# Matmuls of a zero tile ahead of the norm sums and of the grouped first chunks

## The chip, the cores and the metric

The kernel runs on one core of one Trainium2 chip. The time is the device time of one launch in microseconds. The kernel before takes 3053.3 us (median of three runs, 3047.53 to 3057.34). The traces come from single profiled executions.

## The reference, cut to what matters

Two transformer-like blocks of depth 2 over one sequence of 256 tokens and 1024 features, all in float32, one after the other.

```
first_block, for each of 2 layers:
  x = layer_norm(a * x + 0.5 * swiglu(x, w1, w3, w2))
  x = layer_norm(a * x + token_mixing(x))          # gMLP, short conv, MLA and NSA attention, 4 gates, w_o
  x = layer_norm(a * x + cross_attention(x, mem))  # 4 heads of 128, 256 memory rows
  x = layer_norm(a * x + 0.5 * swiglu(x, w1, w3, w2))

second_block, for each of 2 layers:
  x = x + 0.5 * swiglu(rmsnorm(x), w1, w3, w2)
  x = x + mixer(rmsnorm(x))       # layer 0: gated linear attention (GLA) + RG-LRU, layer 1: HGRN2
  x = x + 0.5 * swiglu(rmsnorm(x), w1, w3, w2)
  x = x + sigmoid(rmsnorm(x) @ ple_gate) * (p @ ple_proj)
x = rmsnorm(x)
```

So there are 8 norms with a mean (layer norms), and 9 without (root mean square), and 8 feed-forward networks of width 2816.

## The kernel before, in words

The five engines run five instruction streams that meet through semaphores. Activations lie with features on partitions: `X` is 8 chunks of 128 features by 256 tokens.

**Precision.** A product of float32 numbers is made of three matmuls: each operand is split into a high part (rounded to fp32r) and a low part (the rest), and high x high, high x low and low x high are summed (lines 395, 398, 399 in `three`, or 425, 428, 431 in `together`). `XH` and `XL` are the parts of the activations, `wh` and `wl` those of the weights; `BH` and `BL` hold other activations.

**The stream of weights.** SP loads blocks of 128x1024 into a ring of 6 (`raw`). For each block ACT writes the high part (line 998), POOL the low part in two halves (lines 360, 361, `lo_done`), into a ring of 4. TensorE's `weights()` waits for `lo_done`. The first matmul of a block tells ACT (`block_begun`) that an older one's place is free. A block is used by 24 matmuls.

**PSUM.** `R` has four banks, which `claim()` hands out in turn, waiting until the bank's chunk of four claims ago was taken (`bank_taken`). `Y` has the other four.

**A dense chunk** (`dense`): one block, 8 slices of the features, 3 matmuls each. **The first two or three chunks after a norm** are made by `together`: it waits for two or three blocks and claims as many banks, and then, slice by slice, waits for that slice of the activations (`ready(k)`) and multiplies it into all of them. It is called 18 times: at the start of the 8 feed-forward networks (2 chunks), of the 2 token mixers, the 2 cross attentions, and of the GLA and the HGRN mixer (3 chunks), at the output projections of these last two (3 chunks, from `BH`), and at the 2 gates with `ple_gate` (2 chunks).

**A norm.** TensorE sums over the partitions with a matrix of ones (`stats`, line 520; each such float32 matmul stands as two records in the trace). A norm with a mean has two sums: of `X`, whose result DVE subtracts (line 1664), and of the squares, which ACT writes (line 1091). A norm without has the second alone. Then ACT takes logarithm and exponential for the reciprocal root (lines 1082, 1083), DVE sharpens it (1655 to 1658), and for each of 8 slices DVE scales (1685), adds the bias where there is one (1693), ACT rounds the high part (1101) and DVE subtracts for the low part (1682), which releases `ready(k)`. `norm` on TensorE has places for work between: in the cross attention's norm two chunks of memory keys between the sums (`mem_keys`), more keys and the values behind them (`mem_values`); at the gates the projection of `p` behind the sum.

**Feed-forward.** `ffn` first writes zeros to the four banks of `Y` (line 490: matmuls of the zero tile `ZB`, 128x512 in bf16), then calls `together`, then loops over two up-projections and one down-projection per 128 hidden features. DVE adds the result to `X` (line 1640).

Each engine's order is that of the code; nothing is reordered by a scheduler.

Of the kernel before, what the change touches and what calls it, by code (L numbers as in the profile page):

```python
# [21 lines left out]
P = 128  # L22
# [23 lines left out]
Z_UP, UP_CHUNKS = 21, 14  # L46
Z_GATES = 4 * DC

RAW = 6
SPLIT = 4  # L50
BODY = 12
# [150 lines left out]
def build_program(nc, stream, small, table, masks, mix_w, mix_b, wcmp, x_in, mem_in, p_in, out):  # L202
# [4 lines left out]
    with ctx:  # L207
        def sb(name, shape, dt=F32):
            return ctx.enter_context(nc.sbuf_tensor(name, shape, dt))

        def sem(name):
            return ctx.enter_context(nc.semaphore(name))

        raw = sb("raw", [P, RAW, 1024])
        wh = sb("wh", [P, SPLIT, 1024], F32R)
# [19 lines left out]
        ZB = sb("ZB", [P, 512], BF16)  # L235
# [21 lines left out]

        raw_landed = [sem(f"raw_landed{i}") for i in range(RAW)]
        hi_done, lo_done, block_begun = sem("hi_done"), sem("lo_done"), sem("block_begun")
# [73 lines left out]
        def _(sp):  # L333
# [3 lines left out]
            sp.dma_start(X[:, :, :], x_in).then_inc(x_landed, 16)  # L337
            for n in range(RAW):
                sp.dma_start(raw[:, n, :], stream[n]).then_inc(raw_landed[n], 16)
            trips = (NB - RAW) // RAW  # L340
            with sp.Fori(0, trips) as it:
                for j in range(RAW):

                    sp.wait_ge(lo_done, it * RAW + (j + 1))
                    sp.dma_start(raw[:, j, :], stream[it * RAW + (RAW + j)]).then_inc(raw_landed[j], 16)
# [28 lines left out]
        def _(pe):  # L374
# [3 lines left out]
            def claim():  # L378

                m = t.n["chunk"]  # L380
                t.up("chunk")
                b = m % RING
                if m >= RING:
                    pe.wait_ge(bank_taken[b], t.value(("round", b)))
                t.up(("round", b))
                return R[:, b, :]

            def weights():
                n = t.n["block"]
                pe.wait_ge(lo_done, t.up("block"))  # L390
                return n % SPLIT
# [23 lines left out]
            def together(n, hi, lo, ready):  # L415

                slots, outs = [], []
                for _ in range(n):
                    slots.append(weights())
                    outs.append(claim())  # L420
                for k in range(DC):
                    ready(k)
                    for j, (s, o) in enumerate(zip(slots, outs)):
                        w = (slice(None), s, slice(k * P, k * P + P))
                        i = pe.matmul(o[:, 0:T], wh[w], hi[:, k, :], start=k == 0, stop=False, skip_group_check=True)  # L425
                        if k == 0 and j == 0:
                            i.then_inc(block_begun, 1)
                        i = pe.matmul(o[:, 0:T], wh[w], lo[:, k, :], start=False, stop=False, skip_group_check=True)  # L428
                        if k == DC - 1 and j > 0:
                            i.then_inc(block_begun, 1)  # L430
                        i = pe.matmul(o[:, 0:T], wl[w], hi[:, k, :], start=False, stop=k == DC - 1, skip_group_check=True)  # L431
                        if k == DC - 1:
                            i.then_inc(chunk_ready, 1)
# [52 lines left out]
            def ffn(ready):  # L486

                for b in range(4):

                    pe.matmul(Y[:, b, :], ZB[:, 0:P], ZB[:, :], start=True, stop=False, skip_group_check=True)  # L490

                def up_pair():
                    dense(XH, XL)
                    dense(XH, XL)

                def down(f, end=None):
                    from_dve()
                    s = weights()
                    for c in range(DC):
                        three(Y[:, c // 2, (c % 2) * T:(c % 2) * T + T], (slice(None), s, slice(c * P, c * P + P)),  # L500
                              HH[:, f % 2, :], HL[:, f % 2, :], False, False, begins=c == 0,
                              end=end if c % 2 == 1 else None)

                together(2, XH, XL, ready)
                with pe.Fori(0, (FC - 2) // 4) as it:
                    t.enter(it, {"block": BODY, "chunk": 8, dve_pe: 4, **{("round", b): 2 for b in range(RING)}})
                    for j in range(4):
                        up_pair()
                        down(j)
                    t.leave((FC - 2) // 4)  # L510
                up_pair()
                down(FC - 2)
                down(FC - 1, end=y_ready)

            def stats(n, wait):

                o = claim()
                for c in range(n[0]):
                    wait(c)
                    i = pe.matmul(o[:, 0:T], ONES, n[1](c), start=c == 0, stop=c == n[0] - 1, skip_group_check=True)  # L520
                i.then_inc(chunk_ready, 1)

            def norm(n, src, mean, wait=None, centring=None, scaling=None):
                if mean:
                    stats((n, src), wait)
                if centring is not None:
                    centring()
                stats((n, lambda c: W8[:, c, :]), lambda c: from_act())
                if scaling is not None:
                    scaling()  # L530
# [53 lines left out]
            def mixer(l):  # L584
# [90 lines left out]
                def aside(c):  # L675
# [39 lines left out]
                    if c == 32:  # L715
                        token_mix()

                together(3, XH, XL, split_ready)
                for c in range(3, Z_N):
                    dense(XH, XL)  # L720
# [27 lines left out]
            def cross():  # L748
                together(3, XH, XL, split_ready)
                dense(XH, XL)  # L750
                from_act()
                attention([cross_unit(h) for h in range(4)], lambda u: None)
                from_dve()
                first = t.n["chunk"]
                for _ in range(4):
                    dense(BH, BL, k_tiles=4)
                return first
# [1620 lines left out]
```

## Time and profile before

| | |
|---|---|
| median of three runs | 3053.3 us |
| the three runs | 3047.53, 3053.3, 3057.34 us |
| the profiled execution | 3047.86 us |
| its span, first to last instruction | 3046.1 us |
| mean granted clock of TensorE | 0.968 |
| TensorE busy | 2811.2 us, 92% |
| POOL, DVE, ACT busy | 2195.0, 1392.3, 1380.0 us |

The granted clock is 1.00 at 2.4 GHz and 0.50 at 1.2 GHz; it has these two levels in this trace, and the mean tells how much of the span was at which. A busy time of TensorE counts records whose ends are modelled and which overlap, so the distance from start to start tells the rate, not the length of one record. In a timeline the bracket behind an instruction is the idle time of its engine just before it, and what ended it; an instruction without a bracket followed its predecessor.

### The profile page before, as it was taken

The page shows a single profiled execution, that of the slowest core. Times are in us where ns is not written, and L with a number is a line of the kernel's source. Part 1 is how long each engine was busy: PE and PEld are TensorE (multiplying, and loading weights), DVE is VectorE, ACT ScalarE, POOL GpSimd, SP SyncE. Part 2 cuts the span into 40 slices and gives each one's busy share as a digit, 9 for nine tenths or more (in the row PEclk, how much of TensorE's full clock was granted, in tenths as well). Part 3 has the DMA queues.
Part 4 walks back from the last instruction along what each step waited for, and adds up shares of the span by engine and source line. Part 5 has one row for each costly group of instructions (what it writes and reads, how often), then busy time and mean ns, then how long its engine had stood idle before and what let it go on. Part 6 is the DMA issues. An engine that isn't in the chain of part 4 may idle for free.

```text
span 3046.1 us, 59381 instructions
## 1 busy us (share of the span) xinstructions
PE 2811.2 (92%) x21920; PEld 2687.0 (88%) x21920; DVE 1392.3 (46%) x2271; ACT 1380.0 (45%) x2018; POOL 2195.0 (72%) x1680
## 2 busy tenths in 40 slices
PE   6999999978999999999979998998799899988997
PEld 6999988868998989898868997997799899888996
DVE  3345424644345344524544344347533633654335
ACT  3444444444444444455444444445444544555444
POOL 6976655655996966565746986977699599766994
PEclk9999999999999999899999998999899999999998
DMA  5544433433554544343424553543355355433551
GB/s 206 186 166 145 136 120 123 139 111 110 181 184 140 179 145 163 125 138 112 146 90 132 182 169 118 182 156 125 119 189 181 123 187 180 151 127 133 187 185 63
DMA packets 122403, 451.83 MB, mean 148 GB/s; under 512 B 13586, under 2 KB 13586, under 8 KB 121364
## 3 DMA queue, kind: packets, MB, share of 16 engines
q1 hardware_dynamic: 120960, 441.43, 43.7%
q10 hardware_dynamic: 1300, 8.39, 0.7%
q8 instruction: 102, 1.67, 0.2%
q14 instruction: 41, 0.34, 0.0%
HBM read 448.72 MB, written 1.05 MB: 148 GB/s over the span
## 4 chain that ended last, share of the span: by engine, by line
POOL 58%; issue 30%; PE 9%; DVE 1%; POOLq 1%; ACT 1%; DVEq 0%; ACTq 0%
POOL wl L361 29%; POOL wl L360 29%; PE R L395 2%; PE R L398 2%; PE R L399 2%; PE R L520 1%; PE Y L395 1%; PE Y L398 1%; PE Y L399 1%; POOLq L366 0%; DVE W L1685 0%; PE R L425 0%; PE R L428 0%; PE R L431 0%; DVE XL L1682 0%
## 5 line engine op out<-in xcount | busy, mean ns | idle before, releaser
L360 POOL TENSOR_TENSOR wl<-raw,wh 128x512 fp32r<-128x512 f32 x836 | 1105.0, 1322 | 824.1 <-ACT wh L998 810.3
L998 ACT ACTIVATE wh<-raw 128x1024 fp32r<-128x1024 f32 x836 | 883.5, 1058 | 814.6 <-PE R L395 489.9
L395 PE MATMUL R<-XH,wh 128*128 128x256 f32 x4216 | 1216.5, 289 | 13.3 <-POOL wl L361 6.0
L398 PE MATMUL R<-XL,wh 128*128 128x256 f32 x4216 | 1201.6, 285 | 0.0
L399 PE MATMUL R<-XH,wl 128*128 128x256 f32 x4216 | 1200.9, 285 | 0.0
L361 POOL TENSOR_TENSOR wl<-raw,wh 128x512 fp32r<-128x512 f32 x836 | 1136.4, 1359 | 0.0
L395 PEld LDWEIGHTS R<-XH,wh 128*128 128x128 f32 x4216 | 817.4, 194 | 30.4 <-issue 14.7
L398 PEld LDWEIGHTS R<-XL,wh 128*128 128x128 f32 x4216 | 817.6, 194 | 1.7 <-issue 1.0
L399 PEld LDWEIGHTS R<-XH,wl 128*128 128x128 f32 x4216 | 817.1, 194 | 0.0
L395 PE MATMUL Y<-BH,wh 128*128 128x256 f32 x1408 | 400.0, 284 | 0.9
L398 PE MATMUL Y<-BL,wh 128*128 128x256 f32 x1408 | 399.2, 284 | 0.0
L399 PE MATMUL Y<-BH,wl 128*128 128x256 f32 x1408 | 399.2, 284 | 0.0
L1580 DVE SCALAR_TENSOR_TENSOR M<-M,R 128x256 f32<-128x256 f32 x176 | 74.2, 421 | 561.8 <-ACT M L1056 560.5
L395 PEld LDWEIGHTS Y<-BH,wh 128*128 128x128 f32 x1408 | 270.8, 192 | 2.5 <-DVE BL L1584 2.5
L399 PEld LDWEIGHTS Y<-BH,wl 128*128 128x128 f32 x1408 | 270.8, 192 | 0.0
L398 PEld LDWEIGHTS Y<-BL,wh 128*128 128x128 f32 x1408 | 270.8, 192 | 0.0
L1584 DVE TENSOR_TENSOR BL<-W,BH 128x256 fp32r<-128x256 f32 x176 | 247.1, 1404 | 6.0
L1582 DVE SCALAR_TENSOR_TENSOR W<-M,R 128x256 f32<-128x256 f32 x176 | 74.2, 422 | 327.9 <-PE R L399 327.6
L1056 ACT ACTIVATE M<-R 128x256 f32<-128x256 f32 x176 | 67.4, 383 | 294.6 <-PE R L399 277.8
L425 PE MATMUL R<-XH,wh 128*128 128x256 f32 x304 | 101.9, 335 | 89.1 <-DVE XL L1682 51.0
L395 PE MATMUL R<-BH,wh 128*128 128x256 f32 x544 | 159.4, 293 | 16.3 <-ACT M L1129 5.2
L1583 DVE CAST BH<-W 128x256 fp32r<-128x256 f32 x176 | 168.5, 957 | 6.0
(359 smaller groups left out, 3188.4 us busy)
## 6 DMA issues: line engine op xcount, KB each, us to landing
raw<-in_stream SPq DMA_DIRECT2D x836, 512.0 KB, 3.3
G<-in_wcmp ACTq DMA_DIRECT2D x2, 2048.0 KB, 7.6
G<-in_mem ACTq DMA_DIRECT2D x2, 1024.0 KB, 6.3
TB<-in_table SPq DMA_DIRECT2D x1, 1312.0 KB, 6.3
X<-in_x SPq DMA_DIRECT2D x1, 1024.0 KB, 8.6
out_dram<-X ACTq DMA_DIRECT2D x1, 1024.0 KB, 3.9
WS<-in_mix_w ACTq DMA_DIRECT2D x2, 256.0 KB
G<-in_p ACTq DMA_DIRECT2D x2, 256.0 KB, 2.6
```

What stands on the lines that cost most here:

```text
L360: pool.tensor_tensor(wl[:, s, 0:512], raw[:, r, 0:512], wh[:, s, 0:512].bitcast(F32), ALU.subtract)
L361: pool.tensor_tensor(wl[:, s, 512:], raw[:, r, 512:], wh[:, s, 512:].bitcast(F32), ALU.subtract).then_inc(lo_done, 1)
L395: i = pe.matmul(o, wh[w], hi, start=start, stop=False, skip_group_check=True)
L398: pe.matmul(o, wh[w], lo, start=False, stop=False, skip_group_check=True)
L399: i = pe.matmul(o, wl[w], hi, start=False, stop=stop, skip_group_check=True)
L425: i = pe.matmul(o[:, 0:T], wh[w], hi[:, k, :], start=k == 0, stop=False, skip_group_check=True)
L998: act.activation(wh[:, n % SPLIT, :], raw[:, n % RAW, :], ACT.Copy).then_inc(hi_done, 1)
L1056: give_dve(act.activation(EB[:, j % 2, :], o[:, 0:T], ACT.Tanh, scale=0.5))
L1580: take(stt(e, e, 1.0, o[:, 0:T], ALU.add, ALU.mult), m)
L1582: take(stt(h, e, 0.5 * scale, o[:, 0:T], ALU.mult, ALU.mult), m)
L1583: step(dve.tensor_copy(HH[:, b, :], h))
L1584: give_pe(tt_(HL[:, b, :], h, HH[:, b, :].bitcast(F32), ALU.subtract))
```

## The change

Two places on TensorE get matmuls that multiply the zero tile by itself. In `together`, behind the waits for the weights and the claims of the banks and ahead of the first `ready(k)`, there are 14 of them, into the first claimed bank. In `stats`, behind the claim and ahead of the wait for the first operand, there are 4, into the claimed bank. Each streams 512 columns of bf16. The first real matmul into a bank starts a new sum, so nothing of them remains. `KEEP_BUSY` is the number for `together`.

```
+KEEP_BUSY = 14
...
                 for _ in range(n):
                     slots.append(weights())
                     outs.append(claim())
+                for _ in range(KEEP_BUSY):
+
+                    pe.matmul(outs[0], ZB[:, 0:P], ZB[:, :], start=True, stop=True, skip_group_check=True)
                 for k in range(DC):
                     ready(k)
...
                 o = claim()
                 for c in range(n[0]):
+                    if c == 0:
+                        for _ in range(4):
+                            pe.matmul(o, ZB[:, 0:P], ZB[:, :], start=True, stop=True, skip_group_check=True)
                     wait(c)
                     i = pe.matmul(o[:, 0:T], ONES, n[1](c), start=c == 0, stop=c == n[0] - 1, skip_group_check=True)
```

Lines behind the insertions move: 395 to 399 become 396 to 400, 425, 428, 431 become 429, 432, 435, line 490 becomes 494, and 520 becomes 527. The new matmuls are on lines 424 and 525.

TensorE's order at the end of the first feed-forward network and through the first norm, before. `TB` holds the matrix of ones, `W8` the squares; what an instruction waits for stands behind it.

```order
L399 MATMUL Y<-BH,wl 128x256
L520 MATMUL R<-X,TB 128x256 [waits dve_pe,bank_taken0]
L520 MATMUL R<-X,TB 128x256 [waits dve_pe] x7
L520 MATMUL R<-W8,TB 128x256 [waits act_pe,bank_taken1]
L520 MATMUL R<-W8,TB 128x256 [waits act_pe] x7
L425 MATMUL R<-XH,wh 128x256 [waits lo_done,bank_taken3,bank_taken0,dve_pe,bank_taken2]
L428 MATMUL R<-XL,wh 128x256
L431 MATMUL R<-XH,wl 128x256
```

The same place with the change:

```order
L400 MATMUL Y<-BH,wl 128x256
L525 MATMUL R<-ZB 128x512 [waits bank_taken0]
L525 MATMUL R<-ZB 128x512 x3
L527 MATMUL R<-X,TB 128x256 [waits dve_pe] x8
L525 MATMUL R<-ZB 128x512 [waits bank_taken1]
L525 MATMUL R<-ZB 128x512 x3
L527 MATMUL R<-W8,TB 128x256 [waits act_pe] x8
L424 MATMUL R<-ZB 128x512 [waits bank_taken3,lo_done,bank_taken0,bank_taken2]
L424 MATMUL R<-ZB 128x512 x13
L429 MATMUL R<-XH,wh 128x256 [waits dve_pe]
L432 MATMUL R<-XL,wh 128x256
L435 MATMUL R<-XH,wl 128x256
```

The waits for banks and weights have moved from the first real matmul to the first of the zero tile; the first real one keeps the wait for its operand alone.

TensorE's order at the output projection of the GLA mixer with the change (before, the first matmul of `BH` has all these waits, and follows the last one of `XH` at once):

```order
L396 MATMUL R<-XH,wh 128x256
L399 MATMUL R<-XL,wh 128x256
L400 MATMUL R<-XH,wl 128x256
L424 MATMUL R<-ZB 128x512 [waits bank_taken2,lo_done,bank_taken3,bank_taken1]
L424 MATMUL R<-ZB 128x512 x13
L429 MATMUL R<-BH,wh 128x256 [waits outs_split]
L432 MATMUL R<-BL,wh 128x256
L435 MATMUL R<-BH,wl 128x256
```

Here too the fourteen stand behind `lo_done` of the third block and ahead of the wait for the activations, `outs_split`.

## Rows read from the trace of the kernel before

**Rows 1.** The page: busy time, share of the span and instructions of each engine.
```profile
PE 2811.2 (92%) x21920; PEld 2687.0 (88%) x21920; DVE 1392.3 (46%) x2271; ACT 1380.0 (45%) x2018; POOL 2195.0 (72%) x1680
```

**Rows 2.** Waits of TensorE: waiting line, releaser: us in total, times, longest.
```profile
PE R L425 <- DVE XL L1682: 51.0, 20, 5.3
PE R L425 <- POOL wl L361: 27.7, 3, 10.3
```

**Rows 3.** Line 490's instructions: duration ns least/median/greatest, first and last start.
```profile
L490 PE MATMUL Y<-ZB x32: 378/379/632, 9.6 to 2787.5; 128*128 128x512 bf16 x32
```

**Rows 4.** Timeline: start us, us, engine, line, operation, count [idle before <-releaser].
```profile
9.62 1.87 PE L490 MATMUL Y<-ZB 128*128 128x512 bf16 x4 [9.62 <-ACT CMSK L1463]
...
2424.66 1.03 PE L490 MATMUL Y<-ZB 128*128 128x512 bf16 x4
```

**Rows 5.** Timeline of TensorE in the first norm, behind the first feed-forward network.
```profile
217.90 3.62 PE L520 MATMUL R<-X,TB 128*128 128x256 f32 x16
222.64 3.94 PE L520 MATMUL R<-W,TB 128*128 128x256 f32 x16 [1.13 <-ACT W L1091]
...
231.85 0.56 PE L425 MATMUL R<-XH,wh 128*128 128x256 f32 x1 [5.28 <-DVE XL L1682]
```

**Rows 6.** Timeline of TensorE in the norm ahead of the cross attention.
```profile
618.91 3.62 PE L520 MATMUL R<-X,TB 128*128 128x256 f32 x16
...
628.11 1.24 PE L520 MATMUL R<-W,TB 128*128 128x256 f32 x5
```

**Rows 7.** Timeline of ACT and TensorE in a norm without a mean.
```profile
2377.88 3.56 ACT L1091 ACTIVATE W<-X 128x256 f32<-128x256 f32 x8
...
2378.44 3.75 PE L520 MATMUL R<-W,TB 128*128 128x256 f32 x16 [0.28 <-ACT W L1091]
```

**Rows 8.** Timeline where weights or a bank come last, or nearly.
```profile
656.51 0.55 PE L425 MATMUL R<-XH,wh 128*128 128x256 f32 x1 [10.26 <-POOL wl L361]
...
2148.31 1.71 POOL L361 TENSOR_TENSOR wl<-raw,wh 128x512 fp32r<-128x512 f32 x1
...
2150.71 0.55 PE L425 MATMUL R<-BH,wh 128*128 128x256 f32 x1 [15.08 <-DVE BL L1629]
...
2394.00 0.36 PE L425 MATMUL R<-XH,wh 128*128 128x256 f32 x1 [1.53 <-ACT M L1129]
```

**Rows 9.** Stretches: us, busy time of each engine (count), PEclk, DMA share, GB/s.
```profile
656.50:661.40 4.90, 4.89 (x23) 4.90 (x24) 0.00 (x0) 1.06 (x1) 2.50 (x2) 0.50 0.35 107
661.40:667.50 6.10, 6.10 (x53) 6.10 (x53) 0.00 (x0) 0.64 (x2) 0.00 (x0) 1.00 0.28 89
```

**Rows 10.** Timeline inside a feed-forward group behind a norm with a mean.
```profile
725.63 0.39 PE L425 MATMUL R<-XH,wh 128*128 128x256 f32 x1 [0.39 <-DVE XL L1682]
...
727.00 0.39 PE L425 MATMUL R<-XH,wh 128*128 128x256 f32 x1 [0.39 <-DVE XL L1682]
```

**Rows 11.** Timeline of TensorE at the start.
```profile
25.41 0.55 PE L425 MATMUL R<-XH,wh 128*128 128x256 f32 x1 [13.92 <-DVE XL L2163]
```

**Rows 12.** A stretch behind it, in the first group.
```profile
26.50:29.90 3.40, 3.40 (x18) 3.40 (x18) 0.00 (x0) 0.00 (x0) 0.00 (x0) 1.00 0.04 17
```

**Rows 13.** Timeline of the first chunks of the GLA mixer.
```profile
2048.90 0.55 PE L425 MATMUL R<-XH,wh 128*128 128x256 f32 x1 [4.56 <-DVE XL L1682]
...
2057.11 1.29 POOL L361 TENSOR_TENSOR wl<-raw,wh 128x512 fp32r<-128x512 f32 x1
...
2059.85 0.28 PE L395 MATMUL R<-XH,wh 128*128 128x256 f32 x1
```

**Rows 14.** Timeline of TensorE, the sum of the last norm.
```profile
3026.62 5.38 PE L520 MATMUL R<-W,TB 128*128 128x256 f32 x16 [2.39 <-ACT W L1091]
```

**Rows 15.** A stretch inside that sum.
```profile
3026.80:3030.20 3.40, 3.40 (x9) 2.69 (x9) 0.00 (x0) 2.62 (x7) 0.00 (x0) 0.50 0.02 5
```

**Rows 16.** Stretches in a token mixer, around small matmuls of the compressed attention.
```profile
343.94:347.35 3.41, 3.41 (x30) 3.19 (x29) 0.90 (x4) 0.47 (x1) 2.75 (x3) 1.00 0.73 240
347.35:350.77 3.42, 3.42 (x17) 3.28 (x17) 0.90 (x4) 0.05 (x1) 0.00 (x0) 0.50 0.43 155
```

More of the change, by code:

```diff
@@ L47 @@
 Z_GATES = 4 * DC
+KEEP_BUSY = 14
 RAW = 6
@@ L420, in together @@
                     outs.append(claim())
+                for _ in range(KEEP_BUSY):
+                    pe.matmul(outs[0], ZB[:, 0:P], ZB[:, :], start=True, stop=True, skip_group_check=True)
                 for k in range(DC):
@@ L518, in stats @@
                 for c in range(n[0]):
+                    if c == 0:
+                        for _ in range(4):
+                            pe.matmul(o, ZB[:, 0:P], ZB[:, :], start=True, stop=True, skip_group_check=True)
                     wait(c)
```

## The prediction

> **What bounds the kernel now.** I read the page's engine line first: TensorE is busy for 2811.2 of 3046.1 us, POOL for 72%, DVE and ACT for less than half [rows 1]. In the feed-forward stages the matmuls follow each other without a gap, so time lost there by TensorE is lost to the kernel. Then the waits of TensorE: the first matmul of the "together" groups (line 425) waits 51.0 us in 20 waits for the low part of the activations, and 27.7 us in three waits for POOL's low part of the weights [rows 2]. Those idle times are where the new matmuls are meant to stand. Then, group by group in the timeline, two questions: what ended the wait, and does TensorE or another engine set the pace behind it.
>
> **What is added.** 352 matmuls of a 128x512 bf16 zero tile: 14 in each of 18 together groups, 4 in each of 25 sums over the features. Nothing is removed, no other engine gets an instruction. The kernel has 32 matmuls of exactly this form (line 490), 379 ns each by the record [rows 3]; a row of four takes 1.03 us at full clock and 1.87 us at its start at the low one [rows 4], so one more costs (1.03 - 0.38) / 3 = 0.217 us, and cold about (1.87 - 0.63) / 3 = 0.41 us, with the longest record of [rows 3] for the last. Four cost 0.87 us warm, fourteen 3.0 us warm and 5.8 us cold.
>
> **The sums, by kind.** (a) Eight sums of the chunks before a mean is taken off, with no idle time ahead: TensorE comes straight from its last projection, and the sum runs at its own rate, 3.62 us for 16 records [rows 5, 6]. The four matmuls stand on the path, and DVE, ACT and the second sum wait for the result. 8 x 0.87. The two sums of squares behind the memory keys (628.1 and its twin in layer 1) also start with no idle time [rows 6], 2 x 0.87. Together 8.7 us. (b) The other six sums of squares start after 1.13 us of idle time [rows 5]; 0.87 us fits: 0. If a hand-over eats that cover, 0.2 us each. (c) Six sums of the root-mean-square norms start 0.28 us after TensorE stops, and ACT's squares set the pace: eight in 3.56 us from 2377.88, the sum 3.75 us from 2378.44 [rows 7]. Last squares end at 2381.44. The added four can be issued at about 2378.0, the sum then starts at 2378.87 and its 3.62 us end at 2382.5 and some hundredths, instead of 2382.19: with the drain about 0.45 us later. 6 x 0.45 = 2.7 us. (d) The first such norm, after 10.8 us of idle time, now issues its four only when DVE is done; its sum runs cold anyway. I take 0, between -1 and +1.
>
> **The together groups.** The code waits for the two or three blocks of weights and for the banks, then issues the fourteen, then waits for the activations. So all depends on which wait ended last. In six of the 18 groups the weights or a bank come last, or nearly: 656.5, its twin at 1561 and the HGRN output projection at 2757.4 are released by POOL; the gates at 2394.0 and 2999.5 by ACT emptying a bank; at 2150.7 the activations came last, but POOL's third block was done only at 2148.31 + 1.71 = 2150.02 [rows 8]. There the long idle time holds nothing: the fourteen start when the real ones would have. Behind them TensorE sets the pace: 72 matmuls, 23 of them at clock 0.50 in 4.90 us, 53 at clock 1.00 in 6.10 us, 0.213 and 0.115 us apart [rows 9]. The time at the low clock after the start stays, but part of it is now spent on zeros, so what is lost is their warm price, 3.0 us; at 2150 0.2 us less for the earlier start. 5 x 3.0 + 2.8 = 17.8 us. The upper bound is the cold price with nothing given back, 5.8 each where the group starts cold (four groups): 11 us more. The lower bound is that the low clock ends so much sooner by phase that a group gets back its 1.5 to 2 us: some 7 us less. I take 17.8, which the count of rows gives.
>
> In the other twelve the activations come last, 3.6 to 5.3 us after TensorE stopped [rows 5], and later still at the start; 3.0 us fit: 0, and the idle time falls to 0.6 to 2.3 us. The clock, which falls to 0.50 in most of them, should then mostly stay. But what is that worth? Behind a norm with a mean the group still waits 0.39 us for DVE at 725.63 and again at 727.00 [rows 10]: DVE's steps of 1.37 us a slice are longer than 9 warm matmuls (1.04) and than 6 cold ones (1.28). The four feed-forward groups of the second half fall behind DVE in the cold part and catch up behind it: I give all four together 0.5 us.
>
> **Where the clock pays.** At the start the first real matmul comes after 13.92 us of idle time [rows 11]. Behind it 18 records touch a stretch of 3.40 us [rows 12], where 53 touch 6.10 at full clock [rows 9], so though the column reads 1.00 this is the low rate; it lasts from 25.41 to 29.9, 21 matmuls at 0.213 instead of 0.115: -2.05 us, if zeros fill the end of the idle time. The GLA group from 2048.90 has 24 of its 72 cold, and TensorE sets its pace, with no wait inside; but the next block of weights is ready at 2058.40 and the next matmul stood at 2059.85 [rows 13]: at most -1.35. Its twin at 2630: -0.6. In the final norm the sum starts after 2.39 us of idle time, its clock is 0.50 from 3026.8 on, and it takes 5.38 instead of 3.75 us [rows 14, 15]; four zeros leave 1.5 us of idle time: -1.6; the same at 2419: -1.4. Sum -7.0, with the feed-forward groups -7.5.
>
> **Sum.** 8.7 + 2.7 + 17.8 - 7.5 = +21.7 us. The profiled execution took 3047.86 us, so 3069.6. That execution is 5.4 us below the median of the three timed ones; the mean of all four is 3051.5. I shift by that 3.6 and forecast 3073 us.
>
> **Two rules of the Trainium skill.** Clock and work: from 343.94 to 347.35 TensorE was busy all the time, its last third with 16-column matmuls and small masks, and the clock was 0.50 from 347.35 on [rows 16]. So being busy by the record is not enough. The Trainium skill, "TensorE: Matmul & The Clock Gate" (Part 4: PE-mode transpose), says in the same sense that transposes do not count as TensorE being busy the same way; whether matmuls of zeros count, no run here shows. By that rule applied to zeros the -7.5 us would be 0: that is the second rival. Order: the same page (the table at its head, and Part 3: Packing small matmuls) lets TensorE pull only weight loads ahead, while matmuls start and end in program order; no trace here can show the other. By it the fourteen at the six late groups can't be overtaken; without it they would cost nothing and the sum would be 3.9 us.
>
> **Rivals.** First, the held clock counts in full. For it: the 23 cold matmuls behind 656.5 took 4.90 us, and warm they would have taken 23 x 0.115 = 2.65 [rows 9]; if each of the 18 groups got back such a 2.2 us, that is 40 us, and against the costs of 29.2 it leaves -11: 3041 us, faster. It decides if the chain through DVE's low parts shortens when TensorE does; the 0.39 us waits [rows 10] speak against it, and so do groups whose idle time comes after and not before them. Half of it (the pace of the mean norms gives way, the rest not) makes about +6: within 0.3%. Second, the zeros do not hold the clock: costs alone, 29.2 us, 3081. Third, the fourteen at the late groups are paid at the low clock: 11 us more, 3084; for it that all four start cold, against it that in 656.5 to 661.4 the clock came back while TensorE was at work [rows 9], and work on zeros may bring it back as early.
>
> **Numbers.** Forecast 0.60, in its own range 3063 to 3083. Held clock in full, faster: 0.06. Half of it, about no change: 0.13. Zeros without effect on the clock 0.10, cold price 0.11, both slower. About 0.3% (9 us) is what a measurement can tell from no change, so from 3062.5 us on it is slower; of the forecast's share 0.03 fall below that, and 0.01 of the middle case is faster than by 0.3%. Slower 0.78, same 0.15, faster 0.07. The range of 8 in 10 reaches from 3057 to the two dearer rivals: 3089.
>
> **What would show it.** Line 527's first sum after a feed-forward starts 0.9 us later behind its last projection, with zeros of line 525 in between and no idle time. At the attention over the memory (656.5) the zeros of line 424 start right at POOL's release, at clock 0.50, and the first real matmul (line 429) 4 to 5.5 us after it. In the feed-forward groups line 429 still waits for DVE, and the group takes its 9.8 or 7.5 us as before. Mean clock rises from 0.968 to about 0.98 while the span grows. I am wrong if a group with a mean norm becomes shorter, or if the weights at the six late groups come earlier than the zeros.

## The result, and the profile after

The changed kernel takes 3072.8 us (median of 6 runs, 3070.5 to 3078.7), the kernel before beside it 3052.7 us. The ratio is 1.0068, 95% interval 1.0053 to 1.0082: by the ratio slower by 20.8 us (16.2 to 25.0), against a forecast of 3073 us. The profiled execution took 3078.67 us (span 3076.9), the slowest of the six. Its span is 30.8 us longer than that of the profile of before, so some 10 us of that distance are the two executions' own; below, most of them are found.

The page's engine line [rows 1] after the change:

```profile
PE 2885.4 (94%) x22242; PEld 2708.0 (88%) x22272; DVE 1391.0 (45%) x2271; ACT 1380.4 (45%) x2018; POOL 2195.8 (71%) x1680
```

TensorE is busy for 74.2 us more, the others as before; the time grows by far less, so most of the zeros' work fell into idle time. The trace holds 322 records more for 352 added matmuls: some are missing, and a row of zeros that reads x3 or x13 below stands for four or fourteen. The mean granted clock went from 0.968 to 0.971. The waits of TensorE (line, releaser: us in total, times, longest), to be read against [rows 2]:

```profile
PE R L424 <- POOL wl L362: 50.4, 5, 15.0
PE R L429 <- DVE XL L1689: 19.2, 26, 2.2
...
PE R L525 <- DVE X L1697: 10.2, 1, 10.2
```

The wait for DVE's low part at the real matmuls (now line 429) fell from 51.0 to 19.2 us. The wait for POOL did not shrink. It stands at line 424, the zeros: they begin when POOL lets go and not before. Its total grew from 27.7 us because two waits that used to end with DVE are now put down to POOL: that of the GLA output group (15.0 us) and 6.9 us at the start.

The timeline (start us, us, engine, line, operation, count, idle before and its releaser) at the places of [rows 5], [rows 8], [rows 11], [rows 13] and [rows 14]:

```profile
18.15 6.08 PE L424 MATMUL R<-ZB 128*128 128x512 bf16 x14 [6.89 <-POOL wl L362]
25.10 0.39 PE L429 MATMUL R<-XH,wh 128*128 128x256 f32 x1 [0.86 <-DVE XL L2170]
...
215.86 0.81 PE L525 MATMUL R<-ZB 128*128 128x512 bf16 x3
216.51 3.62 PE L527 MATMUL R<-X,TB 128*128 128x256 f32 x16
219.97 1.03 PE L525 MATMUL R<-ZB 128*128 128x512 bf16 x4
221.16 4.03 PE L527 MATMUL R<-W,TB 128*128 128x256 f32 x16 [0.17 <-ACT W L1098]
...
660.24 5.70 PE L424 MATMUL R<-ZB 128*128 128x512 bf16 x13 [10.51 <-POOL wl L362]
665.43 0.63 PE L429 MATMUL R<-XH,wh 128*128 128x256 f32 x1
...
728.06 0.39 PE L429 MATMUL R<-XH,wh 128*128 128x256 f32 x1 [1.30 <-DVE XL L1689]
...
2058.99 0.81 PE L525 MATMUL R<-ZB 128*128 128x512 bf16 x3
2059.64 3.62 PE L527 MATMUL R<-W,TB 128*128 128x256 f32 x16
...
2414.91 5.59 PE L424 MATMUL R<-ZB 128*128 128x512 bf16 x13 [2.14 <-ACT M L1136]
2420.10 0.52 PE L429 MATMUL R<-XH,wh 128*128 128x256 f32 x1
...
3058.96 3.83 PE L527 MATMUL R<-W,TB 128*128 128x256 f32 x16 [1.42 <-ACT W L1098]
```

Read from the top: at the start the fourteen take 6.08 us, the idle time before the real matmul fell from 13.92 to 0.86 us, and the group behind it was over after 6.01 us instead of 7.97. The first sum behind a feed-forward network has zeros in front and no idle time. The second has its four in the wait that was there: 0.17 us are left of 1.13. At the cross attention the fourteen start at POOL's release and the real matmul comes 5.19 us later. Behind norms with a mean (728.06) DVE is still waited for. The last sum takes 3.83 instead of 5.38 us.

### The profile page after: what moved, and what is told of

It is laid out like the page before. It is cut to its first block, busy times and chain, and to the rows that moved or that the text cites. A ratio compares the mean times of both kernels' runs of the same rounds, so it can differ in the third digit from the quotient of the medians.

```text
span 3076.9 us, 60031 instructions
## 1 busy us (share of the span) xinstructions
PE 2885.4 (94%) x22242; PEld 2708.0 (88%) x22272; DVE 1391.0 (45%) x2271; ACT 1380.4 (45%) x2018; POOL 2195.8 (71%) x1680
## 4 chain that ended last, share of the span: by engine, by line
POOL 58%; issue 30%; PE 9%; DVE 1%; POOLq 1%; ACT 0%; DVEq 0%; ACTq 0%
POOL wl L362 29%; POOL wl L361 29%; PE R L396 2%; PE R L400 2%; PE R L399 2%; PE Y L396 1%; PE Y L400 1%; PE Y L399 1%; PE R L527 1%; POOLq L367 0%; DVE W L1692 0%; PE R L429 0%; PE R L424 0%; PE R L432 0%; PE R L435 0%
## 5 line engine op out<-in xcount | busy, mean ns | idle before, releaser
L396 PE MATMUL R<-XH,wh 128*128 128x256 f32 x4216 | 1214.6, 288 | 13.9 <-POOL wl L362 6.3
L396 PEld LDWEIGHTS R<-XH,wh 128*128 128x128 f32 x4216 | 816.3, 194 | 30.8 <-issue 14.7
L1587 DVE SCALAR_TENSOR_TENSOR M<-M,R 128x256 f32<-128x256 f32 x176 | 74.2, 421 | 560.9 <-ACT M L1063 559.6
L1589 DVE SCALAR_TENSOR_TENSOR W<-M,R 128x256 f32<-128x256 f32 x176 | 74.2, 421 | 328.2 <-PE R L400 327.9
L399 PE MATMUL R<-BL,wh 128*128 128x256 f32 x544 | 156.8, 288 | 0.0
```

What stands on the lines that cost most here:

```text
L396: i = pe.matmul(o, wh[w], hi, start=start, stop=False, skip_group_check=True)
L399: pe.matmul(o, wh[w], lo, start=False, stop=False, skip_group_check=True)
L1587: take(stt(e, e, 1.0, o[:, 0:T], ALU.add, ALU.mult), m)
L1589: take(stt(h, e, 0.5 * scale, o[:, 0:T], ALU.mult, ALU.mult), m)
```

## The experiments

All are edits of the changed kernel; each ratio is against the kernel before in the same series (3048.2, 3050.0 and 3050.2 us; one per mille is 3.05 us). "Zeros" are the added matmuls. To give single places their own numbers, a parameter `busy` (zeros behind the waits for weights and banks) was added to `together` and `stats`, and `ahead` to `together`: zeros behind the first bank's wait, ahead of the weights.

**Sums only.** `e1_sums_only`:

```
-KEEP_BUSY = 14
+KEEP_BUSY = 0
```

> The four zero matmuls ahead of each of the 25 sums stay, the fourteen in the 18 together groups go. My theory (a zero matmul costs its 0.217 us wherever TensorE sets the pace, and nothing in idle time): 10 sums x 0.87 and 6 x 0.30 cost 10.5 us, the two sums behind the gates get back 1.3 and 1.5 us; so +7.7 us against before, 3061, ratio 1.0025, and in the trace every sum behind a feed-forward starts 0.87 us later. Rival 1 (the groups carry the whole cost, the sums' zeros are hidden): -3 us. Rival 2 (zeros do not hold the clock): +10.5 us, and the sums behind the gates still at clock 0.50.

Measured 1.0034 (1.0021 to 1.0048), 10.4 us. In its trace the first sums behind the feed-forward networks and both sums of the norm with the memory keys start 0.87 us later each, as forecast, and the two sums behind the gates are back at full clock. The expected 1.0025 lies inside the interval.

**Groups only.** `e2_groups_only`:

```
-                    if c == 0:
-                        for _ in range(4):
-                            pe.matmul(o, ZB[:, 0:P], ZB[:, :], ...)
```

> The fourteen in the 18 together groups stay, the four ahead of the sums go. My theory: six late groups cost 3.0 us each (17.8), twelve nothing, the clock gives back 2.0 at the start, 2.0 in the GLA and HGRN first groups, 0.5 elsewhere: +13.3 us, 3066, ratio 1.0044. In the trace after, the late groups cost between 1.3 and 5.6 us each, so where the low clock lies may add up to 5 us. Rival 1 (held clock counts in full): under 0. Rival 2 (cold price, 5.8 us each in the late groups): +24. The sum of this and of the run with the sums alone should be the whole change, +20 us, if the two parts don't touch.

Measured 1.0045 (1.0031 to 1.0059), 13.7 us, where 1.0044 was expected. The sums at 2419 and 3026 take 5.38 us, so the fourteen in the groups do nothing for them: what they gain elsewhere comes with the four zeros ahead of them. The two parts make 24.1 us, the whole 20.8; the intervals allow that.

**Zeros in idle time only.** `e3_idle_only`: fourteen in the twelve groups whose activations come last, four ahead of the sums at 2419 and 3026, none elsewhere.

```
-                together(3, XH, XL, split_ready)              # cross; GLA, HGRN output; gates alike
+                together(3, XH, XL, split_ready, busy=0)
...
-                norm(DC, None, False)                         # first of each layer, and the last
+                norm(DC, None, False, busy=4 if l else 0)
```

> Zeros only where TensorE has idle time to hide them: fourteen in the twelve together groups whose weights are early, four ahead of the two sums behind the gates; none in the six late groups, none ahead of the other 23 sums. My theory: no cost and the whole gain, -7 us against before, 3046, ratio 0.9977, with the slices of the groups behind norms with a mean still at DVE's pace and no shorter. Rival 1 (held clock counts in full, 2.2 us in each of the twelve): -26 us, 0.9915. Rival 2 (zeros do not hold the clock): 0, 1.0000.

Measured 0.9972 (0.9961 to 0.9983), median 3039.2 us: 8.5 us faster than the kernel before, 7 expected. The same kernel in another series, `e11_idle_again`:

> The third experiment's kernel once more, beside the two that split it, to see whether its time is that of the sum of the two: theory -7 to -9 us, ratio 0.997 to 0.9977, close to the five places alone. Rival (its 3039.2 us was a lucky set of runs, as the fourth and seventh experiments, with the same zeros and 40 more, lie at 0.998): -5 us, 0.9984.

Measured 0.9973 (0.9964 to 0.9982), median 3040.4 us. So the time is repeatable, and this is the fastest of the versions tried, by median. It beats both kernels, by a little: 0.27%. Its trace at the final norm:

```profile
3016.71 1.04 PE L530 MATMUL R<-ZB 128*128 128x512 bf16 x4
3019.16 3.83 PE L532 MATMUL R<-W,TB 128*128 128x256 f32 x16 [1.42 <-ACT W L1103]
```

The zeros end 1.42 us before the sum, which ran at full clock all the same.

**Where that gain is made.** `e9_five_sites` has zeros only at the start, at the first groups of GLA and HGRN and ahead of the two sums; `e10_nine_sites` has those of the other nine places.

```
-            def ffn(ready):
+            def ffn(ready, busy=0):
...
-            ffn(first_split)
+            ffn(first_split, KEEP_BUSY)    # e10: 0 here, KEEP_BUSY in the seven later ones
```

> Zeros only at the five places where the prediction counts a gain from the clock: fourteen at the start group, at the first groups of GLA and HGRN, four ahead of the sums at 2419 and 3026. Theory (the gain is made where TensorE sets the pace behind the wait): all of the prediction's -7.0 us, ratio 0.9977, the same as the third experiment within 2 us. Rival (the gain is spread over all groups whose clock is held): the five are a third of the places, so -2 to -4 us.

> The other nine places of the third experiment: fourteen zeros in the two token mixers' first groups behind a norm with a mean and in the seven feed-forward groups after the first. The held clock is the same as in the third experiment, but DVE's low parts set the pace behind it. Theory: -0.5 us, ratio 1.000, within what can be measured of no change. Rival (the gain is spread over all groups): -5 to -8 us.

Measured 0.9982 (0.9974 to 0.9991) for the five, -5.5 us, and 0.9989 (0.9980 to 0.9998) for the nine, -3.4 us. Together 8.9 us, about the time of all fourteen places. The five seem to carry more than the nine, though the two intervals overlap; it is less than the 7.0 us that were expected of them, and the nine gain more than the 0.5. The trace of the five shows their list: -2.4 us by the end of the first group, -2.0 by the end of GLA's output group, sums of 3.84 and 3.83 us. That of the nine shows no gain at the groups behind a mean norm. It is the trace of its slowest execution (3054.75 us, with the low stretch in the mixer that is shown below), and nearly all that it does gain lies at places that have no zeros: the last sum

```profile
3035.04 3.74 PE L532 MATMUL R<-W,TB 128*128 128x256 f32 x16 [2.39 <-ACT W L1103]
```

runs at full clock after the same 2.39 us of idle time behind which it took 5.38 us before [rows 14], and the gates at 3009.39 take 5.99 us where they took 7.49. The reverse happens too: in the third experiment's trace the gates at 2389.52, without zeros, take 7.48 us where they took 5.99, which cancels the gain of the sum behind them. So a low stretch moves on or off a place by itself, and one trace can't say what the zeros of one place are worth. Over all traces the sums' four zeros still stand out: with them 16 sums of 16, in eight kernels, take 3.83 or 3.84 us; without them nine of ten, in five kernels, take 5.18 to 5.38. How the nine gain what they gain stays open.

**The late groups alone.** `e5_late_only`, and `e6_late_doubled` with 28 for 14:

```
-                together(3, XH, XL, split_ready, busy=0)      # the six late groups
+                together(3, XH, XL, split_ready, busy=KEEP_BUSY)   # e6: 2 * KEEP_BUSY
```

> Fourteen zero matmuls only in the six groups whose weights or activations come late against the wait that the zeros stand behind (both cross attentions, the output projections of GLA and HGRN, the gates at 2394 and 2999), none anywhere else. Theory (behind a wait that ends last, the zeros are work on the path, and what the group regains of clock is small): the prediction's own term, six groups, +17.8 us, so about 3066 on a before of 3048.2, ratio 1.0058. From the trace of the changed kernel, where the zeros of four of the six ran partly at the low clock, up to +23. Rival (the 24 cold matmuls at a group's start are paid back by the zeros that warm the clock): 14 zeros at 0.43 us cost 6.0, the group gets 2.0 shorter; but when only 3.0 of zeros run before the clock rises, 1 or less net for each, +6 in all, ratio 1.002.

> As the one before, but 28 zeros in each of the six late groups. Theory (full price, nothing more to regain once the clock is up): the second fourteen cost 14 x 0.217 = 3.0 us in each, +18.2 over the run with fourteen, at full clock, so about +36 against the kernel before, ratio 1.012. Rival (the zeros overlap with something else on the path, such as DVE or POOL making the next chunk's operands, so that a part is hidden): clearly less than +18 over the run with fourteen, and the idle time of TensorE inside those groups falls.

Measured 1.0062 (1.0050 to 1.0075), 18.9 us, where 17.8 stood in the sum; and 1.0116 (1.0101 to 1.0131), 35.4 us. The second fourteen cost 16.5 us, about full price (18.2). Timelines at the first cross attention, of fourteen and of twenty-eight:

```profile
656.15 5.54 PE L429 MATMUL R<-ZB 128*128 128x512 bf16 x14 [10.14 <-POOL wl L362]
...
661.34 0.47 PE L434 MATMUL R<-XH,wh 128*128 128x256 f32 x1
```

```profile
661.14 8.17 PE L429 MATMUL R<-ZB 128*128 128x512 bf16 x28 [10.15 <-POOL wl L362]
```

The idle time, 10.1 us, is the same in both: not one zero went into it. Fourteen take 5.2 us because they start at the low clock, but the real matmuls behind then begin at full clock (0.12 us apart, where [rows 9] has 0.213), and what is left by the next sum is 3.06 us. Twenty-eight take 8.17 us, 2.6 more. That settles two alternatives of the prediction: a filler at the late groups is not hidden (that would have left 3.9 us in all), and what it costs beyond the warm price is given back.

**Into the long waits instead.** If the late groups' idle time is 10 us long, zeros could stand ahead of the weights' wait. `e4_ahead_of_weights` is the third experiment with 40 such zeros at both cross attentions and 28 at HGRN's output projection; `e7_cross_ahead` has the 40 only.

```
                 slots, outs = [], []
+                if ahead:
+                    outs.append(claim())
+                for _ in range(ahead):
+                    pe.matmul(outs[0], ZB[:, 0:P], ZB[:, :], ...)
                 for _ in range(n):
                     slots.append(weights())
```

> As the run with zeros in idle time alone, and in three of the late groups the zeros stand behind the first claim of a bank and ahead of the wait for the weights: 40 at the two cross attentions (8.7 of 10.3 us idle), 28 at the HGRN output projection (6.1 of 7.2 us idle). My theory: the same matmuls that cost 3.0 us behind the wait cost nothing ahead of it and hold the clock: the three groups take 8.9 us instead of 11.0, 11.0 and 10.4, so -7 - 5.7 = -12.7 us against before, 3040, ratio 0.9958. Rival 1 (what costs is the zero work itself, not its place): 108 zeros at 0.217 us make +23 us. Rival 2 (no effect on the clock): 0.

> The third experiment (zeros in idle time only) with the 40 zeros ahead of the weights' wait added at both cross attentions, and not at HGRN's output projection. Theory from the traces of the last two: the groups there get 2.4 and 1.8 us shorter, and the attention behind, whose small matmuls then meet a low clock of 17 us in place of 3.4, gives it back: same as the third experiment within 2 us or slower, up to +4, so 3039 to 3043. Rival (the loss of the fourth experiment came from HGRN's 28 zeros): 4 us faster than the third, 3035.

Measured 0.9981 (0.9972 to 0.9990), median 3043.6 us, and 0.9980 (0.9970 to 0.9990), median 3044.7 us. The fourth experiment's expectation is missed: 0.9958 was expected, and it isn't faster than the third. The seventh came out as expected: by its ratio 2.4 us slower than the third, where up to 4 were allowed and the rival had it 4 us faster. The trace of the fourth shows that the zeros did what they should:

```profile
643.54 8.81 PE L422 MATMUL R<-ZB 128*128 128x512 bf16 x40
653.96 0.36 PE L434 MATMUL R<-XH,wh 128*128 128x256 f32 x1 [1.61 <-POOL wl L362]
...
2743.92 6.22 PE L422 MATMUL R<-ZB 128*128 128x512 bf16 x28
...
2751.27 0.36 PE L434 MATMUL R<-BH,wh 128*128 128x256 f32 x1 [1.14 <-POOL wl L362]
...
2757.19 0.39 PE L434 MATMUL R<-BH,wh 128*128 128x256 f32 x1 [1.37 <-DVE BL L1641]
```

At the cross attention the group starts at full clock and gains some 2.2 us. In the attention behind it the two traces part. Stretches (us; busy time of each engine; clock) of the fourth experiment, then the same of the third:

```profile
672.43:675.84 3.41, 3.41 (x11) 2.88 (x10) 0.81 (x2) 0.60 (x1) 0.00 (x0) 0.50 0.41 151
682.67:696.32 13.65, 10.33 (x40) 8.64 (x39) 3.61 (x6) 1.94 (x3) 2.52 (x2) 0.50 0.04 11
```

```profile
672.43:675.84 3.41, 1.24 (x8) 1.07 (x8) 1.90 (x6) 2.66 (x9) 1.07 (x1) 1.00 0.75 246
682.67:696.32 13.65, 9.58 (x57) 8.67 (x57) 4.76 (x10) 3.31 (x4) 3.34 (x3) 0.87 0.11 37
```

With the group warm the clock is low for all 13.65 us from 682.67, and 40 matmuls are done where the third experiment does 57; the attention takes 4.3 us longer, and by the next norm the fourth is 1.9 us behind. The seventh has the same two low stretches, moved by 4.4 us. In both traces of the third kernel the first is missing, and of the second there are 3.4 us. So at the first cross attention the gain was paid back about twice within 50 us, in two kernels out of two. At the second the group gains 2.2 us again, and the attention behind it gives back 1.3. Both places together lose 1.2 us in either trace; what makes the clock fall there is not shown. The fourth's trace is of one of its faster executions (3040.14 us) and ends level with the third's, so it doesn't explain the last 2 to 3 us between the two kernels. At HGRN's output nothing is gained for another reason: the next slice of the activations then has to be waited for, 1.37 us for DVE. TensorE only gets to the wait sooner.

**And two longer waits.** `e8_long_waits`, the third with

```
-                norm(DC, None, False, busy=4 if l else 0)
+                norm(DC, None, False, busy=4 if l else 44)
...
-                together(3, BH, BL, piece_ready, busy=0)           # GLA output
+                together(3, BH, BL, piece_ready, busy=0, ahead=64)
```

> The third experiment, and the two longest waits left at a low clock filled too: 44 zeros ahead of the first sum of squares of the token half (10.8 us idle before it, sum 6.28 us against 3.83 at full clock) and 64 ahead of the weights at GLA's output projection (15.1 us idle, 16 matmuls at 0.21 us in place of 0.12 behind it). Theory (the time of the matmuls that run at the low clock is given back where the sum has no other pace): -2.4 for the sum, whose operands are there all at once, and between 0 and -1.5 for the group, whose pieces DVE makes: 3035.3 to 3036.8 where the third has 3039.2. Rival (a low stretch kept off here comes later at the expense of the matmuls behind it, as in the fourth experiment): 3039 or more.

Measured 1.0014 (1.0005 to 1.0023), median 3055.6 us: some 12 to 13 us slower than the third, where 3 less were expected. The theory didn't have this; the rival's "3039 or more" holds the number, but its reason, a low stretch that comes later, isn't what the trace shows:

```profile
1835.64 12.46 PE L530 MATMUL R<-ZB 128*128 128x512 bf16 x44 [10.18 <-DVE X L1702]
1847.94 3.62 PE L532 MATMUL R<-W,TB 128*128 128x256 f32 x16
...
2144.26 15.67 PE L422 MATMUL R<-ZB 128*128 128x512 bf16 x64 [2.63 <-DVE Z L2038]
...
2163.18 0.38 PE L434 MATMUL R<-BH,wh 128*128 128x256 f32 x1 [1.09 <-DVE BL L1641]
```

The 10.8 us before the first sum of squares of the token half are not free for zeros. TensorE stands in `from_dve(DC)`, the wait ahead of the norm, and the zeros come behind it: 44 of them on the path for 12.3 us. ACT, for which the profile of before had the wait, is only 0.6 us later than DVE, so the sum starts 11.7 us later than in the third experiment. It then takes 3.62 us instead of 6.28, 2.7 less, where 2.4 were expected. The 64 at GLA's output start 2.6 us late, run longer than the wait they fill (15.67 us, eight of them at the low clock), and the group behind them waits 1.09 us for DVE's next part: 1.7 us lost. 11.7 - 2.7 + 1.7 makes 10.7 of the 12 to 13 us. That kernel gave its matmuls one of the highest clocks of all (0.977 in its best runs) and is slower than the kernel before.

## Why the prediction was right

**Sum by sum.** (a) The eight first sums and the two behind the memory keys: 0.87 us each was forecast, and 0.87 was measured at each. (b) The six second sums: forecast 0; they start 0.17 us after their zeros where there was 1.13 us of idle time. Against the first sum that is 0.09 us earlier, and they run 0.09 us longer (4.03 for 3.94): 0. (c) The sums of the other norms: forecast 0.45, and they start 0.44 us later, but run 3.62 instead of 3.75 us, so 0.31 are left. (d) The first of these: forecast 0, measured 1.09 before it and 0.87 back, as its sum takes 5.37 instead of 6.24 us: 0.2.

**Late groups.** The largest term, 17.8 us, was measured by itself at 18.9 (15 to 23). It rests on reading which wait ended last, and the row at 660.24 is that reading come true. The even share of 3.0 us did not come true: by the end of the group the trace of the changed kernel has 3.7 and 2.3 us at the two cross attentions, 5.6 at the gates from 2414.91, where all thirteen recorded zeros ran at the low clock, and 1.3 at the last gates. That these sizes average to the 3 us of the forecast is in part luck.

**What the clock gives.** -7.5 us forecast, -8.5 and -8.2 measured in the two series of the third experiment. The split was less good: the five places that were to bring 7.0 us brought 5.5 (2.7 to 7.9), the nine that were to bring 0.5 brought 3.4 (0.6 to 6.1), and that the two misses cancel is luck. The single sizes were close where they were made: -2.0 for -2.05 at the start, -1.34 and -1.55 for -1.4 and -1.6 at the two sums. The first groups of GLA and HGRN became 2.2 and 1.5 us shorter, but then TensorE waits 0.74 us for POOL's next block, and the next chunk starts 1.40 and 0.65 us earlier, where the prediction's reading of [rows 13] gave -1.35 and -0.6.

One of these is less sure than it looks. Eight kernels have the fourteen at the start, and in six traces the group takes 6.0 us; in those of the seventh and eighth experiments it takes 7.5. A stretch of it in the seventh, and in the third:

```profile
25.00:28.20 3.20, 3.20 (x15) 3.20 (x16) 0.00 (x0) 0.00 (x0) 0.00 (x0) 0.50 0.17 68
```

```profile
25.00:28.20 3.20, 3.20 (x27) 3.20 (x27) 0.00 (x0) 0.00 (x0) 0.00 (x0) 1.00 0.19 76
```

The idle time behind the zeros is 2.04 us in the seventh and 2.37 us in the third, so it is not a longer wait that lets the clock fall; why it falls there is open.

The groups of two chunks behind a norm with a mean take 9.92 us, where they took 9.83 and started cold: DVE's pace, as forecast, and with it the first rival (3041 us) falls. So does the second (3081 us, zeros don't hold the clock): the third experiment would have shown no gain. The third rival, the cold price with nothing given back, would have made the late groups' 17.8 us into 29; 18.9 were measured.

**Sum.** 8.7 for the sums with a mean, 1.9 and 0.2 for the others, 18.9, -8.4: 21.2 us, where 21.7 was forecast and 20.8 is measured. The interval of the change is 4.4 us to either side, so that the forecast of 3073 us meets 3072.8 to 0.2 us is luck; that the terms and their causes hold is not.

**What was not right.** The mean clock was to reach about 0.98; it is 0.971 to 0.974. The late groups' zeros explain little of that, for the third experiment has none there and is at 0.975 in most runs. The small matmuls of [rows 16] begin at 344.37, so they fill nearly the whole stretch of 3.41 us and not its last third; what the prediction took from the rows, that a busy TensorE can lose the clock, stands. The profile of the changed kernel also holds 3.1 us that no part of the change pays for. TensorE in a mixer of small matmuls, before and after (timeline):

```profile
283.97 3.75 PE L626 MATMUL Y<-G,O 64*16 64x64 f32 x128
```

```profile
281.95 6.08 PE L633 MATMUL Y<-G,O 64*16 64x64 f32 x128
```

And the stretch from 280.05 in the profile of before and in that of after:

```profile
280.05:286.88 6.83, 6.83 (x234) 6.72 (x234) 4.95 (x13) 1.25 (x3) 1.48 (x2) 1.00 0.49 158
```

```profile
280.05:286.88 6.83, 6.83 (x134) 6.79 (x132) 3.90 (x12) 0.00 (x0) 0.00 (x0) 0.50 0.26 82
```

TensorE has no idle time in either, and the clock is 1.00 in one and 0.50 in the other. The profiles of the first, sixth, ninth and tenth experiments have this low stretch too, the fifth and seventh have half of it, the second, third, fourth, eighth and eleventh have none, and no arrangement of zeros is common to those that have it. The same trace has three more such places, by the time from one group's end to the next sum or wait: the attention behind each cross attention's first chunks is 1.4 and 1.6 us longer than before, beyond its zeros, and the HGRN mixer some 3 us, with low stretches at 2703.5 and 2754.7 where the profile of before has none. Together these four are about 9 of the 10 us that set the profiled execution apart. I count them as belonging to the execution and not to the change; they may be a part of the 4 to 12 us by which runs of one kernel differ here, but no run was made to settle it.

## What to carry to other kernels

Work that fills a wait must be issued behind the wait's predecessor and ahead of what is waited for: behind the last wait it costs its full time, however long the idle time in front. So look up for each place which wait ends last, and which ones stand before the filler (banks, an engine's hand-over), since the profile names only the last. Holding the clock is worth time where TensorE sets the pace behind the wait; there it brought 0.6 to 2.0 us a place. Zeros only in waits that end behind them make a kernel that is 0.27% faster, where zeros everywhere make it 0.68% slower. And read a place's gain from several traces: low stretches move from one kernel, or one execution, to the next, and are worth as much as the gain that is looked for.

## What the runs showed of the hardware

- Matmuls of a zero tile can hold the granted clock, and it can rise while they run (behind fourteen of them from 656.15 the real matmuls are 0.12 us apart, without them 0.213). Four before a sum leave it at 3.83 us instead of 5.38, with 1.42 us of idle time between, in 16 cases of 16. Fourteen before the first group did it in six traces of eight.
- One 128x512 bf16 zero matmul costs 0.217 us at full clock by [rows 4] and 0.215 by the fourteen in 3.18 us before the feed-forward groups of the token half ((3.18 - 0.38) / 13), and 0.43 at the low clock (in the trace of the eighth experiment, from 1836.0 on, the zeros' weight loads start 0.43 us apart). The Trainium skill, "TensorE: Matmul & The Clock Gate" (Part 1, the HAM clock gate), gives the start-to-start time as the columns over the clock and 2.5 ns more when warm; the traces agree with both.
- A busy TensorE can be at the low clock: 6.83 us without idle time, 128 matmuls of 64x64 in 6.08 us instead of 3.75. The kernel before has a shorter such stretch, 3.42 us [rows 16]. No rule for it was found.
- A higher mean clock is no measure of a gain: 0.977 at 3050 us in the eighth experiment, 0.968 at 3048 us in the kernel before.
